# A hybrid encoder layer: the first quarter of x and the first weight tile loaded and split in quarter-megabyte blocks

## The chip, the cores and the metric

One core of one Trainium2 chip runs the whole layer. The metric is device microseconds of one execution, taken as the median of several runs.

## What is computed

The reference, cut to what matters here (batch 1, 256 tokens, width 2048, depth 1):

```
xn = rmsnorm(x, norm_pre_w)                  # 256 x 2048
h  = xn @ w_in                               # 2048 x 13312, split into q, k, v, z, gates ...
...                                          # windowed attention with bias, HGRN2 forward and backward
y  = g_a * (o_a @ w_branch[:1024]) + g_b * (o_b @ w_branch[1024:])
x  = x + rmsnorm(y @ w_out, norm_post_w)
```

The products are kept near float32: each float32 operand is split into a high part, rounded to the type the matmul takes in one pass, and a low part, the remainder. A product is then hi x hi + hi x lo + lo x hi.

## The kernel before, in words

Weights come as "tiles" of 1 MB through the four slots of `raw`. SP issues every weight load in one fixed order (`load`, line 292); a load into a slot waits until VectorE has split the tile that lay there (`lo_ready`). ScalarE copies each half tile (128 x 1024) into `w_hi` (`split_hi`, line 440, the activation is line 447), VectorE subtracts to make `w_lo` (`split_lo`, line 706, line 710). `w_hi` and `w_lo` hold four halves; ScalarE writes a half only when TensorE has counted enough used halves in `half_used`. Each engine runs its own program in order, and all of them meet only at semaphores.

The first 16 tiles are the early tiles. They compute v and i for all heads with the tokens on the rows: tile n covers four of x's sixteen 128-column blocks (k = 4r to 4r+3, r = n mod 4) and 512 output columns, and tiles 0 to 3 together make the first column block of v. Each half tile has two k, two token tiles t and three products each: 12 matmuls of 128 x 512 (lines 1226 to 1228, in `early_tile`, line 1198). In this stage x is used unnormalised apart from the column weights; the row scale is applied when the sums are taken.

x comes from memory with tokens on the partitions. TensorE turns it, 128 x 128 at a time, into PSUM (`turn_x`, line 1186; line 1190). ScalarE makes the high part from PSUM, with the norm's column weight (`first_hi` for k = 0 and 1 by token tile, line 553 and 556; `x_hi` for both token tiles at once, line 559 and 561), and VectorE the low part (`first_lo` line 994, `x_lo` line 1000 and 1002).

The start, engine by engine, in the order of each program:

- SP (lines 335 to 342): x's first 1024 columns for t = 0 (512 KB, `load_x`), the first half of tile 0 (512 KB, `early_half`, line 331), the same two for t = 1 and the second half, tile 1 (1 MB), x's second 1024 columns (two of 512 KB), tiles 2 to 15.
- TensorE (lines 1363 to 1375): six dummy products of ones (`warm`, line 1194), the turn of the norm weights, one dummy, eight turns of x for t = 0, five dummies, eight turns for t = 1, the turn of the vector rows (`ps_vec`, line 1373), then `early_tile(0)` to `early_tile(15)`. A dummy shows as two loads and two matmuls in the trace, a turn as one. In tile 1, between the halves, stand the 16 turns of x's second 1024 columns, which wait for `vec_ready` (the bank they go to is the one the vector rows were in).
- ScalarE (lines 591 to 612): the norm weights from PSUM; for each t, `first_hi(t)` and the high split of half t of tile 0; `x_hi` of k = 2 to 7; the copy of the turned vector rows (line 600, waits for `vec_turned`); the split of tile 1; the squares of x's first columns (line 568); tile 2 with x blocks 8 to 11 between; x blocks 12 to 15; the other squares; from there tile n+1 in step n.
- VectorE (lines 1034 to 1061): the same order for the low parts; later, in steps 6 to 15, the scaled and split activations for the main part (`scale_pair`, lines 1024 and 1027, `act_lo`, line 1031; ScalarE's part is `act_hi`, line 583).
- GpSimd makes the masks at the start, and later adds the column window to the attention bias of each head pair (`mask_bias`, line 409), which SP loads within the group's weight loads.

After the early tiles, weights are the stationary operand (`project`, lines 1173 and 1175) for eight groups of ten tiles, eight tail tiles, 16 branch tiles and 16 output tiles.

Of the kernel before, what the change touches and what calls it, by code (L numbers as in the profile page):

```python
# [25 lines left out]
ALU = mybir.AluOpType  # L26
# [6 lines left out]
P = 128  # L33
# [25 lines left out]
WARM_UP = 6  # L59
KEEP_WARM = 5  # L60
NSLOT_Q, NSLOT_K, NSLOT_Z, NSLOT_F, NSLOT_B, NSLOT_HQ, NSLOT_G0, NSLOT_G1, NSLOT_G2, NSLOT_HZ = range(10)
# [32 lines left out]
def encoder_layer(nc, x, norm_pre_w, w_in, b_gate, na_rel_bias, hg_lb_logits, hg_norm_w, w_branch,  # L94
# [5 lines left out]
    with ExitStack() as ctx:  # L100
# [3 lines left out]
        def sem(name):  # L104
            return ctx.enter_context(nc.semaphore(name))
# [61 lines left out]
        def dec_of(level):  # L167
# [18 lines left out]

        first_landed = [sem(f"first_landed{h}") for h in range(2)]
        raw_landed = [sem(f"raw_landed{i}") for i in range(RAW)]
# [7 lines left out]
            sem("vec_landed"), sem("norm_landed"), sem("norm_turned"), sem("norm_ready"))  # L196
        x_landed = [[sem(f"x_landed{side}{t}") for t in range(2)] for side in range(2)]
        block_taken, v_ready, i_ready = sem("block_taken"), sem("v_ready"), sem("i_ready")
        const_step, ones_ready, win_ready = sem("const_step"), sem("ones_ready"), sem("win_ready")
# [91 lines left out]
        def _(sp):  # L291
# [28 lines left out]

            def load_x(side, t):
                half = slice(side * (D // 2), (side + 1) * (D // 2))
                sp.dma_start(x_tok[:, t, half], x[0, t * P:(t + 1) * P, half]).then_inc(x_landed[side][t], 16)

# [5 lines left out]

            def early_half(h):
                dst = raw[:, 0, 1024 * h:1024 * (h + 1)].rearrange("p (k c) -> p k c", k=2)
                sp.dma_start(dst, w_in_v[:, 2 * h:2 * h + 2, V_TILE * P:V_TILE * P + 512]).then_inc(first_landed[h], 16)

            for t in range(2):
                load_x(0, t)
                early_half(t)
            early(1)
            for t in range(2):
                load_x(1, t)  # L340
            for n in range(2, N_PRE):
# [97 lines left out]
        def _(act):  # L439
            def split_hi(n, r, landed, h):  # L440

                if isinstance(n, int) and n == 0:
                    act.wait_ge(first_landed[h], 16)
                elif h == 0:
# [97 lines left out]
            def group(g0, p, first):  # L542
                g = g0 + p
                for s in range(IN_SLOTS):
# [6 lines left out]
                    take_part(place(g0, p, s)[0], s % 2)  # L551

            def first_hi(t):
                act.wait_ge(xt_done, t + 1)
                for k in range(2):
                    nc.scalar.activation(x_hl[:, k, t * P:(t + 1) * P], first_turned[t][:, k * P:(k + 1) * P], ACT.Copy,
                                         scale=norm_w[:, k:k + 1]).then_inc(xhi_ready, 1)
# [6 lines left out]
            def square(side):  # L564
                wait(act, ss_ready, 2 * side)
                for t in range(2):
                    act.wait_ge(x_landed[side][t], 16)
                    nc.scalar.activation(squares[t], x_tok[:, t, side * (D // 2):(side + 1) * (D // 2)], ACT.Square,
                                         accum_out=ssq[:, 2 * side + t:2 * side + t + 1]).then_inc(ss_ready, 1)
# [24 lines left out]
            for t in range(2):  # L594
                first_hi(t)
                split_hi(0, 0, 0, t)
            for k in range(2, 8):
                x_hi(k)
# [103 lines left out]
        def _(dve):  # L702
# [326 lines left out]
            def act_lo(i):  # L1029
                dve.wait_ge(act_hi_ready, i + 1)  # L1030
                nc.vector.tensor_tensor(act_hl[:, 2 * i:2 * i + 2, T:2 * T], x_pair[i % 2],
                                        act_hl[:, 2 * i:2 * i + 2, 0:T].bitcast(F32), ALU.subtract).then_inc(act_ready, 1)

            dve.wait_ge(norm_ready, 1)
            for t in range(2):
                first_lo(t)
                split_lo(0, 0, t)
            for k in range(2, 8):
                x_lo(k)
# [120 lines left out]
        def _(pe):  # L1160
# [24 lines left out]

            def turn_x(side, t):

                pe.wait_ge(x_landed[side][t], 16)
                for k in range(8 * side, 8 * side + 8):
                    ins = nc.tensor.transpose(turned(k, t), x_tok[:, t, k * P:(k + 1) * P], block[:, 0, :])  # L1190
                    if k == 1 or (t == 1 and k % 2 == 1):
                        ins.then_inc(xt_done, 1)

            def warm(count):
                for _ in range(count):
                    nc.tensor.matmul(ps_proj[1][:, 0:P], ones[:, :], ones[:, :], start=True, stop=True)

            def early_tile(n):

                c, r = n // 4, n % 4  # L1200
                for h in range(2):
                    if (n, h) == (1, 1):
                        pe.wait_ge(vec_ready, 1)
                        for t in range(2):
                            turn_x(1, t)
                    if (n, h) == (5, 1):
# [4 lines left out]
                        ins.then_inc(rows_ready, 1)  # L1211
                    if c == 0 and n + h > 0:
                        pe.wait_ge(xn_ready, 4 * r + 2 * h + 4)
                    elif c > 1 and r == 0 and h == 0:
                        pe.wait_ge(block_taken, 2 * (c - 1))
                    pe.wait_ge(lo_ready, n * 2 + h + 1)
                    i = (2 * r + h) % HALVES
                    for t in range(2):
                        if n + h == 0:
                            pe.wait_ge(xn_ready, 2 * t + 2)  # L1220
# [147 lines left out]
            warm(1)  # L1368
            turn_x(0, 0)
            warm(KEEP_WARM)  # L1370
            turn_x(0, 1)
            pe.wait_ge(vec_landed, 3 * 16)
            nc.tensor.transpose(ps_vec, vec_rows[:, :], block[0:72, 0, 0:72]).then_inc(vec_turned, 1)
            for n in range(N_PRE):
                early_tile(n)
# [82 lines left out]
```

## Time and profile before

| | |
|---|---|
| median of 3 runs | 840.54 us (840.07 to 840.79) |
| profiled execution | 840.67 us |
| its span on the core | 838.9 us |
| TensorE busy | 826.4 us (99%) |
| VectorE busy | 631.9 us (75%) |
| ScalarE busy | 414.0 us (49%) |
| DMA, mean over the span | 183 GB/s |
| mean granted TensorE clock | 0.997 of full speed |

The span is the time between the first and the last record on the core, and the profiled execution's own time is 1.8 us more. Matmuls overlap one another, so a 128 x 512 product shows some 0.39 us busy while one follows another at 0.23 us. All times in the rows are from the start of the span.

### The profile page before, as it was taken

What the parts mean: (1) busy time and instruction counts of PE and PEld (TensorE: products, weight loads), DVE (VectorE), ACT (ScalarE), POOL (GpSimd) and SP (SyncE); (2) the same over time, 40 slices, a digit from 0 to 9 for tenths busy, and PEclk for the clock granted to TensorE, in tenths of its full rate; (3) what the DMA queues carried; (4) which work ended last, traced back from release to release, by engine and by line L of the source; (5) the groups of instructions that cost most, each with busy time, mean ns of one, the idle gap of its engine ahead of it and who ended that gap; (6) DMA issues with size and microseconds to landing.
All of it is one profiled execution on the core that took longest, in us unless ns stands there. A gap on an engine that the chain in (4) does not pass through costs nothing.

```text
span 838.9 us, 14167 instructions
## 1 busy us (share of the span) xinstructions
PE 826.4 (99%) x5006; PEld 708.3 (84%) x5006; DVE 631.9 (75%) x1053; ACT 414.0 (49%) x706; POOL 40.8 (5%) x48
## 2 busy tenths in 40 slices
PE   8999999999999999999999999999999999999996
PEld 7888788888888888888888888888888888888884
DVE  4767658788888888888888897897785778775443
ACT  6644445445445445445445445435545545544442
POOL 5000100000000000000100000100000000000002
PEclk9999999999999999999999999999999999999998
DMA  9755877666566566566567667656557767676522
GB/s 330 273 186 175 209 190 177 174 183 167 161 193 167 158 192 171 154 187 172 160 180 172 167 172 182 166 165 183 152 158 195 215 186 199 185 267 212 185 106 100
DMA packets 246708, 153.63 MB, mean 183 GB/s; under 512 B 15288, under 2 KB 228368, under 8 KB 246288
## 3 DMA queue, kind: packets, MB, share of 16 engines
q1 hardware_dynamic: 245664, 149.17, 63.0%
q10 hardware_dynamic: 1008, 3.98, 1.2%
q8 instruction: 23, 0.38, 0.2%
q14 instruction: 13, 0.11, 0.0%
HBM read 151.04 MB, written 2.10 MB: 183 GB/s over the span
## 4 chain that ended last, share of the span: by engine, by line
PE 91%; DVE 5%; ACT 2%; DMA 1%; issue 1%; POOL 0%; SPq 0%; POOLq 0%; ACTq 0%; DVEq 0%
PE psum L1173 47%; PE psum L1175 23%; PE psum L1414 3%; PE psum L1416 3%; PE psum L1415 3%; DVE w_lo L710 3%; PE psum L1276 2%; PE psum L1226 1%; PE psum L1228 1%; PE psum L1227 1%; ACT w_hi L447 1%; PE psum L1266 1%; DMA raw<-in_w_in 1%; PE psum L1242 1%; PE psum L1311 1%; PE psum L1255 1%
## 5 line engine op out<-in xcount | busy, mean ns | idle before, releaser
L1173 PE MATMUL psum<-act_hl,w_hi 128*128 128x512 f32 x1408 | 502.6, 401 | 0.0
L1175 PE MATMUL psum<-act_hl,w_lo 128*128 128x256 f32 x1408 | 394.9, 280 | 0.0
L710 DVE TENSOR_TENSOR w_lo<-raw,w_hi 128x1024 fp32r<-128x1024 f32 x272 | 325.1, 1233 | 82.5 <-ACT w_hi L447 82.3
L1173 PEld LDWEIGHTS psum<-act_hl,w_hi 128*128 128x128 f32 x1408 | 264.4, 188 | 64.8
L447 ACT ACTIVATE w_hi<-raw 128x1024 fp32r<-128x1024 f32 x272 | 273.6, 1053 | 40.2 <-PE psum L1416 25.6
L1175 PEld LDWEIGHTS psum<-act_hl,w_lo 128*128 128x128 f32 x1408 | 266.0, 189 | 0.0
L461 ACT ACTIVATE part<-psum 128x256 f32<-128x256 f32 x88 | 33.7, 383 | 218.2 <-PE psum L1175 218.1
L1173 PE MATMUL psum<-branch_hl,w_hi 128*128 128x512 f32 x256 | 90.6, 399 | 0.0
L1175 PE MATMUL psum<-branch_hl,w_lo 128*128 128x256 f32 x256 | 71.9, 281 | 0.0
L1173 PEld LDWEIGHTS psum<-branch_hl,w_hi 128*128 128x128 f32 x256 | 48.1, 188 | 12.0
L1226 PE MATMUL psum<-w_hi,branch_hl 128*128 128x512 f32 x128 | 50.4, 393 | 1.5 <-DVE w_lo L710 0.9
L1414 PE MATMUL psum<-w_hi,act_hl 128*128 128x512 f32 x128 | 49.9, 390 | 0.2 <-DVE w_lo L710 0.2
L1228 PE MATMUL psum<-w_hi,branch_hl 128*128 128x512 f32 x128 | 49.8, 389 | 0.0
L1227 PE MATMUL psum<-w_lo,branch_hl 128*128 128x512 f32 x128 | 49.8, 389 | 0.0
L1415 PE MATMUL psum<-w_lo,act_hl 128*128 128x512 f32 x128 | 49.8, 389 | 0.0
L1416 PE MATMUL psum<-w_hi,act_hl 128*128 128x512 f32 x128 | 49.8, 389 | 0.0
L1175 PEld LDWEIGHTS psum<-branch_hl,w_lo 128*128 128x128 f32 x256 | 48.4, 189 | 0.0
L478 ACT ACTIVATE wide<-wide,small 128x256 f32<-128x256 f32 x32 | 16.0, 502 | 47.3 <-DVE small L750 47.3
L731 DVE TENSOR_TENSOR hg<-psum,part 128x256 f32<-128x256 f32 x32 | 13.6, 425 | 31.7 <-ACT part L461 31.7
L790 DVE TENSOR_TENSOR hg<-hg 128x256 f32<-128x256 f32 x56 | 31.8, 568 | 0.8
L1226 PEld LDWEIGHTS psum<-w_hi,branch_hl 128*128 128x128 f32 x128 | 24.0, 188 | 7.3 <-DVE w_lo L710 1.4
L1414 PEld LDWEIGHTS psum<-w_hi,act_hl 128*128 128x128 f32 x128 | 24.0, 188 | 5.5 <-DVE w_lo L710 0.6
(137 smaller groups left out, 691.1 us busy)
## 6 DMA issues: line engine op xcount, KB each, us to landing
raw<-in_w_in SPq DMA_DIRECT2D x103, 1024.0 KB, 5.7
raw<-in_w_branch SPq DMA_DIRECT2D x16, 1024.0 KB, 6.0
raw<-in_w_out SPq DMA_DIRECT2D x16, 1024.0 KB, 5.1
bias_t<-in_na_rel_bias SPq DMA_DIRECT2D x32, 96.0 KB, 5.9
big<-in_x SPq DMA_DIRECT2D x4, 512.0 KB, 8.5
big<-in_x ACTq DMA_DIRECT2D x2, 1024.0 KB, 6.7
out<-big SPq DMA_DIRECT2D x5, 256.0 KB, 2.7
raw<-in_w_in SPq DMA_DIRECT2D x2, 512.0 KB, 6.7
```

Of the source, the lines that this page charges most:

```text
L447: nc.scalar.activation(w_hi[:, (2 * r + h) % HALVES, :], raw[:, r, 1024 * h:1024 * (h + 1)], ACT.Copy).then_inc(hi_ready, 1)
L461: nc.scalar.activation(part[:, b, :], ps_proj[b][:, T:2 * T], ACT.Copy).then_inc(part_ready, 1)
L710: nc.vector.tensor_tensor(w_lo[:, i, :], raw[:, r, 1024 * h:1024 * (h + 1)], w_hi[:, i, :].bitcast(F32), ALU.subtract).then_inc(lo_ready, 1)
L790: hg_s.done(nc.vector.tensor_tensor(sides(suf_f, pre_b, half), sides(suf_f, pre_b, half), sides(pre_f, suf_b, half, 2 * half - 1, 0, 0), A ...
L1173: nc.tensor.matmul(sums[h][:, :], w_hi[:, i, w], operand[:, k, :], start=first, stop=False, skip_group_check=True)
L1175: ins = nc.tensor.matmul(sums[h][:, 0:T], w_lo[:, i, w], operand[:, k, 0:T], start=False, stop=last, skip_group_check=True)
L1226: nc.tensor.matmul(sums, hi, w_hi[:, i, w], start=(k == 0), stop=False)
L1227: nc.tensor.matmul(sums, hi, w_lo[:, i, w], start=False, stop=False)
L1228: ins = nc.tensor.matmul(sums, lo, w_hi[:, i, w], start=False, stop=(k == KT - 1))
L1414: nc.tensor.matmul(o, hi, w_hi[:, i, w], start=(k == 0), stop=False)
L1415: nc.tensor.matmul(o, hi, w_lo[:, i, w], start=False, stop=False)
L1416: ins = nc.tensor.matmul(o, lo, w_hi[:, i, w], start=False, stop=(k == KT - 1))
```

## The change

x's first 1024 columns are loaded as two pieces per token tile: columns 0 to 511, then 512 to 1023. The first weight tile is loaded as four blocks of one k each (128 x 512, 256 KB). SP's order is: x piece one of t = 0, block 0, x piece one of t = 1, blocks 1, 2, 3, x piece two of t = 0 and of t = 1, tile 1, and the rest as before. ScalarE and VectorE split tile 0 block by block. On TensorE a new function, `first_tile`, takes the place of the turns of the first 1024 columns and of `early_tile(0)`: it turns four k instead of eight, has four dummies instead of five, starts the products of block 0 for t = 0 before t = 1 is turned, and turns k = 4 to 7 of both token tiles between the products of blocks 2 and 3. The turn of the vector rows, which stood ahead of all products, stands behind `first_tile`. On ScalarE the order is `first_hi(0)`, block 0, `first_hi(1)`, block 1, x blocks 2 and 3, weight blocks 2 and 3, x blocks 4 to 7, the vector rows' copy, tile 1. The number of products is the same. The square of x's first columns also waits for the new pieces' semaphores.

```diff
-KEEP_WARM = 5
+KEEP_WARM = 4
+FIRST_K = 4
...
             for t in range(2):
-                load_x(0, t)
-                early_half(t)
+                load_x(0, FIRST_K, t, x_first_landed[t])
+                first_weights(t)
+            for k in range(2, FIRST_K):
+                first_weights(k)
+            for t in range(2):
+                load_x(FIRST_K, 8, t, x_landed[0][t])
             early(1)
             for t in range(2):
-                load_x(1, t)
+                load_x(8, KT, t, x_landed[1][t])
...
+            def first_split_hi(k):
+                act.wait_ge(first_landed[k], 16)
+                nc.scalar.activation(w_hi[:, k // 2, 512 * (k % 2):512 * (k % 2) + 512],
+                                     raw[:, 0, 512 * k:512 * (k + 1)],
+                                     ACT.Copy).then_inc(hi_ready if k % 2 else first_w_hi, 1)
...
             for t in range(2):
                 first_hi(t)
-                split_hi(0, 0, 0, t)
-            for k in range(2, 8):
+                first_split_hi(t)
+            for k in range(2, FIRST_K):
+                x_hi(k)
+            for k in range(2, FIRST_K):
+                first_split_hi(k)
+            for k in range(FIRST_K, 8):
                 x_hi(k)
             act.wait_ge(vec_turned, 1)
...
+            def first_split_lo(k):
+                dve.wait_ge(hi_ready if k % 2 else first_w_hi, k // 2 + 1)
+                half = slice(512 * (k % 2), 512 * (k % 2) + 512)
+                nc.vector.tensor_tensor(w_lo[:, k // 2, half], raw[:, 0, 512 * k:512 * (k + 1)],
+                                        w_hi[:, k // 2, half].bitcast(F32),
+                                        ALU.subtract).then_inc(lo_ready if k % 2 else first_w_lo, 1)
+
             dve.wait_ge(norm_ready, 1)
             for t in range(2):
                 first_lo(t)
-                split_lo(0, 0, t)
-            for k in range(2, 8):
+                first_split_lo(t)
+            for k in range(2, FIRST_K):
+                x_lo(k)
+                first_split_lo(k)
+            for k in range(FIRST_K, 8):
                 x_lo(k)
...
+            def first_products(k, t):
+
+                hi, lo = x_hl[:, k, t * P:(t + 1) * P], x_hl[:, k, T + t * P:T + (t + 1) * P]
+                w = slice((k % 2) * 512, (k % 2 + 1) * 512)
+                pe.wait_ge(hi_ready if k % 2 else first_w_hi, k // 2 + 1)
+                pe.wait_ge(xn_ready, 2 * t + 2 if k < 2 else k + 3)
+                nc.tensor.matmul(bank[4 + t], hi, w_hi[:, k // 2, w], start=(k == 0), stop=False)
+                nc.tensor.matmul(bank[4 + t], lo, w_hi[:, k // 2, w], start=False, stop=False)
+                pe.wait_ge(lo_ready if k % 2 else first_w_lo, k // 2 + 1)
+                return nc.tensor.matmul(bank[4 + t], hi, w_lo[:, k // 2, w], start=False, stop=False)
+
+            def first_tile():
+
+                turn_x(0, FIRST_K, 0, x_first_landed[0])
+                warm(KEEP_WARM)
+                first_products(0, 0)
+                turn_x(0, FIRST_K, 1, x_first_landed[1])
+                first_products(0, 1)
+                for t in range(2):
+                    ins = first_products(1, t)
+                ins.then_inc(half_used, 1)
+                for t in range(2):
+                    first_products(2, t)
+                for t in range(2):
+                    turn_x(FIRST_K, 8, t, x_landed[0][t])
+                for t in range(2):
+                    ins = first_products(3, t)
+                ins.then_inc(half_used, 1)
...
             warm(1)
-            turn_x(0, 0)
-            warm(KEEP_WARM)
-            turn_x(0, 1)
+            first_tile()
             pe.wait_ge(vec_landed, 3 * 16)
             nc.tensor.transpose(ps_vec, vec_rows[:, :], block[0:72, 0, 0:72]).then_inc(vec_turned, 1)
-            for n in range(N_PRE):
+            for n in range(1, N_PRE):
                 early_tile(n)
```

## Rows read from the trace of the kernel before

**Rows 1.** The page: the chain that ended last, share of the span by engine.

```profile
PE 91%; DVE 5%; ACT 2%; DMA 1%; issue 1%; POOL 0%; SPq 0%; POOLq 0%; ACTq 0%; DVEq 0%
```

**Rows 2.** Waits of TensorE, 45 us to the end: us in total, times, longest.

```profile
PE psum L1226 <- DVE w_lo L710: 0.9, 1, 0.9
```

**Rows 3.** TensorE's timeline, first 20 us: start, us, operation, xcount, idle before and releaser.

```profile
1.07 2.64 PEld L1196 LDWEIGHTS psum<-ones 128*128 128x128 f32 x12 [1.07 <-POOL ones L366]
...
4.28 0.39 PEld L1196 LDWEIGHTS psum<-ones 128*128 128x128 f32 x2
4.99 0.86 PEld L1190 LDWEIGHTS psum<-block,big 128*128 128x128 f32 x8 [0.32 <-DMA big<-in_x]
5.82 1.20 PEld L1196 LDWEIGHTS psum<-ones 128*128 128x128 f32 x10
8.53 0.85 PEld L1190 LDWEIGHTS psum<-block,big 128*128 128x128 f32 x8 [1.52 <-DMA big<-in_x]
...
9.51 0.49 PE L1226 MATMUL psum<-w_hi,branch_hl 128*128 128x512 f32 x1
...
13.08 0.50 PE L1226 MATMUL psum<-w_hi,branch_hl 128*128 128x512 f32 x1 [0.54 <-DVE branch_hl L1002]
...
15.84 0.19 PEld L1226 LDWEIGHTS psum<-w_hi,branch_hl 128*128 128x128 f32 x1 [0.17 <-issue]
...
18.48 1.90 PEld L1190 LDWEIGHTS psum<-block,big 128*128 128x128 f32 x16
```

**Rows 4.** ScalarE's timeline, first 21 us.

```profile
5.54 0.63 ACT L556 ACTIVATE branch_hl<-psum,vec 128x128 fp32r<-128x128 f32 x2 [0.96 <-PE psum L1190]
7.14 1.06 ACT L447 ACTIVATE w_hi<-raw 128x1024 fp32r<-128x1024 f32 x1 [0.98 <-DMA raw<-in_w_in]
9.01 0.63 ACT L556 ACTIVATE branch_hl<-psum,vec 128x128 fp32r<-128x128 f32 x2 [0.81 <-PE psum L1190]
...
10.85 2.28 ACT L561 ACTIVATE branch_hl<-psum,vec 128x256 fp32r<-128x256 f32 x6
12.99 0.26 ACT L600 ACTIVATE vec<-psum 128x72 f32<-128x72 f32 x1
13.11 2.04 ACT L447 ACTIVATE w_hi<-raw 128x1024 fp32r<-128x1024 f32 x2
...
17.84 1.06 ACT L447 ACTIVATE w_hi<-raw 128x1024 fp32r<-128x1024 f32 x1 [0.62 <-DMA raw<-in_w_in]
20.00 0.84 ACT L561 ACTIVATE branch_hl<-psum,vec 128x256 fp32r<-128x256 f32 x2 [1.09 <-PE psum L1190]
```

**Rows 5.** VectorE's timeline, first 20 us.

```profile
9.66 0.61 DVE L994 SCALAR_TENSOR_TENSOR branch_hl<-psum,vec,branch_hl 128x128 fp32r<-128x128 f32 x2 [0.21 <-ACT branch_hl L556]
...
14.52 2.34 DVE L710 TENSOR_TENSOR w_lo<-raw,w_hi 128x1024 fp32r<-128x1024 f32 x2
18.94 1.23 DVE L710 TENSOR_TENSOR w_lo<-raw,w_hi 128x1024 fp32r<-128x1024 f32 x1 [2.08 <-ACT w_hi L447]
```

**Rows 6.** SP's queue, one of its first issues: start, us, line.

```profile
1.26 0.42 SPq L333 DMA_DIRECT2D raw<-in_w_in  x1
```

**Rows 7.** Groups by form, 30 to 110 us: xcount | busy, mean ns | idle.

```profile
L1031 DVE TENSOR_TENSOR act_hl<-hg,act_hl 128x512 fp32r<-128x512 f32 x8 | 5.5, 684 | 0.0
L583 ACT ACTIVATE act_hl<-hg 128x512 fp32r<-128x512 f32 x8 | 5.1, 633 | 25.6 <-DVE hg L1027 25.6
```

**Rows 8.** The chain that ended last, in order of time: start, us, what.

```profile
45.60 1.07 ACT w_hi L447
```

**Rows 9.** GpSimd's and VectorE's timelines near 89 us.

```profile
88.86 2.41 POOL L409 TENSOR_TENSOR bias_t<-bias_t,win 128x768 f32<-128x768 f32 x1 [57.50 <-DMA bias_t<-in_na_rel_bias]
...
89.49 2.33 DVE L1024 TENSOR_TENSOR hg<-branch_hl 128x512 f32<-128x512 f32 x1
```

**Rows 10.** Stretches at the end: us, busy by engine, granted clock, DMA share, GB/s.

```profile
830.00:835.00 5.00, 0.64 (x3) 0.19 (x1) 4.08 (x8) 2.39 (x5) 4.28 (x4) 0.89 0.65 227
835.00:839.00 4.00, 0.00 (x0) 0.00 (x0) 0.00 (x0) 0.00 (x0) 0.00 (x0) 0.50 0.69 241
```

More of the change, by code:

```diff
@@ L184, in encoder_layer @@
         x_pair = (hg[:, 0:2, :], hg[:, 2:4, :])
-        first_landed = [sem(f"first_landed{h}") for h in range(2)]
+        first_landed = [sem(f"first_landed{k}") for k in range(FIRST_K)]
+        first_w_hi, first_w_lo = sem("first_w_hi"), sem("first_w_lo")
         raw_landed = [sem(f"raw_landed{i}") for i in range(RAW)]
@@ L197, in encoder_layer @@
         x_landed = [[sem(f"x_landed{side}{t}") for t in range(2)] for side in range(2)]
+        x_first_landed = [sem(f"x_first_landed{t}") for t in range(2)]
         block_taken, v_ready, i_ready = sem("block_taken"), sem("v_ready"), sem("i_ready")
@@ L319, in group, with load_x @@
                     load(r, w_in_v[:, :, cols], n)
-            def load_x(side, t):
-                half = slice(side * (D // 2), (side + 1) * (D // 2))
-                sp.dma_start(x_tok[:, t, half], x[0, t * P:(t + 1) * P, half]).then_inc(x_landed[side][t], 16)
+            def load_x(first_k, last_k, t, landed):
+                cols = slice(first_k * P, last_k * P)
+                sp.dma_start(x_tok[:, t, cols], x[0, t * P:(t + 1) * P, cols]).then_inc(landed, 16)
             def early(n):
@@ L329, in early, with first_weights @@
                 load(r, src, n)
-            def early_half(h):
-                dst = raw[:, 0, 1024 * h:1024 * (h + 1)].rearrange("p (k c) -> p k c", k=2)
-                sp.dma_start(dst, w_in_v[:, 2 * h:2 * h + 2, V_TILE * P:V_TILE * P + 512]).then_inc(first_landed[h], 16)
+            def first_weights(k):
+                sp.dma_start(raw[:, 0, 512 * k:512 * (k + 1)],
+                             w_in_v[:, k, V_TILE * P:V_TILE * P + 512]).then_inc(first_landed[k], 16)
             for t in range(2):
-                load_x(0, t)
-                early_half(t)
+                load_x(0, FIRST_K, t, x_first_landed[t])
[4 more added lines that the diff above has]
+                load_x(FIRST_K, 8, t, x_landed[0][t])
             early(1)
             for t in range(2):
-                load_x(1, t)
+                load_x(8, KT, t, x_landed[1][t])
             for n in range(2, N_PRE):
@@ L440, in split_hi @@
             def split_hi(n, r, landed, h):
-                if isinstance(n, int) and n == 0:
-                    act.wait_ge(first_landed[h], 16)
-                elif h == 0:
+                if h == 0:
                     act.wait_ge(raw_landed[r], landed)
@@ L566, in square @@
                 for t in range(2):
+                    if side == 0:
+                        act.wait_ge(x_first_landed[t], 16)
                     act.wait_ge(x_landed[side][t], 16)
@@ L1184, in turned, with turn_x @@
                 return turn_bank[k // 2][:, c:c + P]
-            def turn_x(side, t):
-                pe.wait_ge(x_landed[side][t], 16)
-                for k in range(8 * side, 8 * side + 8):
+            def turn_x(first_k, last_k, t, landed):
+                pe.wait_ge(landed, 16)
+                for k in range(first_k, last_k):
                     ins = nc.tensor.transpose(turned(k, t), x_tok[:, t, k * P:(k + 1) * P], block[:, 0, :])
@@ L1204, in early_tile @@
                         for t in range(2):
-                            turn_x(1, t)
+                            turn_x(8, KT, t, x_landed[1][t])
                     if (n, h) == (5, 1):
@@ L1211, in early_tile @@
                         ins.then_inc(rows_ready, 1)
-                    if c == 0 and n + h > 0:
+                    if c == 0:
                         pe.wait_ge(xn_ready, 4 * r + 2 * h + 4)
@@ L1218, in early_tile @@
                     for t in range(2):
-                        if n + h == 0:
-                            pe.wait_ge(xn_ready, 2 * t + 2)
                         sums = bank[4 + 2 * (c % 2) + t]
```

## The prediction

> **What bounds the kernel now.** I first read the chain of work that ended last [rows 1]: TensorE carries 91% of it, so the body of the kernel is TensorE's own work. The waits of TensorE from 45 us to the end come next [rows 2]: the longest is one of 0.9 us, and no other matters. So nothing behind the start is slack that could swallow a delay or hide a gain, and the question is when TensorE's unbroken work begins. That is in the timelines of the first 20 us, engine by engine. On TensorE [rows 3] the reader is to see three holes: after the warm-up products (5.82 + 1.20 = 7.02) until the turn of x's second token tile at 8.53; then 12 products from 9.51 that end the first half tile; then 0.54 us until 13.08. From 13.08 twelve products take until 15.84, 0.23 us each, and weight tile 1 begins there with a hole of 0.17. ScalarE [rows 4] and VectorE [rows 5] show what feeds this: the weight half is split high in 1.06 us and low in 1.23 us, and x's column blocks are taken from PSUM in 0.38 us each (six in 2.28).
>
> The first low half of tile 1 is ready near 15.75 (two take 2.34 from 14.52, 1.17 apiece) and tile 1 begins at 15.84: before the change TensorE and the split of tile 1 arrive together. That decides this case. The change may start TensorE earlier, but it pays only if tile 1's split is ready earlier too.
>
> **The first blocks, step by step.** Loading: each old 512 KB transfer becomes 256 KB pieces. The pieces have the 2 KB rows that the weight transfers had; the first 2 MB is the same data, in eight issues for four at some 0.46 us each (0.42 and a short gap) [rows 6], so tile 1's issue is about 1.9 us later; tile 1 is wanted by ScalarE only at 15.5, so this costs nothing.
> - Turn of t=0: TensorE is free at 4.28 + 0.39 = 4.67, and now waits for x to 4.99 [rows 3]. With half the bytes I take 4.75 (bounds 4.67 and 4.99). Four turns replace eight, four dummies five; both lie under the wait for the split.
> - ScalarE takes the two blocks 0.5 us after the turn starts, as it did (8.53 to 9.01, 4.99 to 5.54), in 0.63: 5.25 to 5.88. Then the split of weight block 0. No row has exactly this instruction; the nearest of the same size and types are 0.63 on ScalarE and 0.68 on VectorE [rows 7]. High: 5.85 to 6.48. Low: 6.52 to 7.20.
> - Weight block 0 must have landed by 5.85. Its bytes end where x's first 512 KB ended, which had landed by 4.99, and it is issued some 0.46 later: 5.45. Upper bound: the 7.14 of the old half. I take 5.45, so it is hidden.
> - TensorE: two products from 6.55, the low one at 7.22, then the turn of t=1 at 7.45. Its old chain from turn to blocks ready is 8.53 to 9.66 + 0.61 = 10.27 [rows 3, 5], 1.74; plus 0.05: the products of block 0, t=1, begin at 9.24. Three take 0.80 (3 x 0.23, and 0.11 because the first product after a hole shows 0.50 and not 0.39): 10.04. Block 1's six end at 11.42; its low part is ready at 9.9.
> - ScalarE goes on: x blocks 2 and 3 to 9.95, high of weight blocks 2 and 3 to 11.1; VectorE has low 2 ready at 11.2, low 3 at 12.2. So block 2 runs unhindered, 11.42 to 12.80.
>
> Up to here TensorE has done 18 products of tile 0 by 12.80, where it now has done 12. The new order is better than the old by over a microsecond.
>
> **The step that pays it back.** Now x's second quarter is turned, between blocks 2 and 3: eight turns at 1.90 / 16 = 0.12 [rows 3], to 13.74; block 3's six products end at 15.12. Only then comes the turn of the vector rows, which before stood ahead of all products. ScalarE's program has, in order: x blocks 4 to 7, the copy of the vectors, the split of tile 1. Before, all of x's first half was turned by 9.4, and these ran without a wait to the split at 13.11 [rows 4]. Now:
> - x block 4 needs the sixth turn: 12.80 + 0.70, plus the 0.35 that the old row shows (18.48 + 10 x 0.117 = 19.65, ScalarE at 20.00): 13.85. ScalarE idles from 11.1 to there. Four blocks at 0.38: 15.37.
> - The copy of the vectors needs their turn at 15.12, plus 0.3 us until ScalarE has it: 15.42. Both arrive together, so removing either wait alone would not help.
> - Plus 0.12 for the copy: split of tile 1 at 15.54, where it was 13.11. Low starts 1.10 later (17.84 to 18.94 is such a pair), takes 1.23: 17.87. TensorE begins tile 1 at 17.90.
>
> Queued behind on ScalarE: the squares of x, the split of tile 2, x blocks 8 to 15, all shifted alike. Tile 2's transfer, for which ScalarE now waits until 17.84, is hidden then, but the next thing it needs, x block 8, hangs on TensorE's turn behind tile 1's first half, so nothing is caught up. SP's (the load queue's) issues of tiles 4 and on wait for low splits, and shift with them.
>
> **The sum.** 17.90 - 15.84 = +2.06 us at the start of tile 1. From there to 45.6 TensorE has no hole before; at 45.60 the chain passes to ScalarE, released by TensorE's half tile [rows 8], and ScalarE and VectorE set the pace until the 0.9 us wait. In that stretch the 128x512 add on VectorE at 89.49 took 2.33, where a pass of that size takes 0.68 [rows 7]; it ran beside GpSimd's add at 88.86 [rows 9]. Both are timed by the same chain (SP's loads wait for VectorE's splits), so I let the meeting recur unchanged: 0, bounds -0.95 (the wait gone) to +0.8 (a meeting as costly again). So +2.06: 840.67 becomes 842.7 for a profiled execution (span 838.9 to 841.0), and by the median of 840.54, 842.6.
>
> **The clock.** TensorE would stand idle from about 15.4 to 17.9, longer than any hole of the old start (1.5). At the end of the old trace, with 0.64 us of TensorE work in 830 to 835, the granted clock averaged 0.89; in 835 to 839, with none, it was 0.50, which is the 1.2 GHz level [rows 10]. So it falls after idleness, but not at once. At the start the twelve dummy loads take 0.22 each and the later ten 0.12 [rows 3]: the price of the low level is about double. I take no fall, because the work around the hole is dense. The Trainium skill ("TensorE: Matmul & The Clock Gate", section "HAM oscillation — how this bites in real kernels") says that waits between bursts of matmuls send the clock back to half rate and that every return is paid anew; it speaks against this change. Taken at its word here it gives the third rival's time.
>
> **Rivals.**
> 1. *First landing late.* If block 0 lands at 7.14 as the old half did, its split, the turn of t=1 and all that follows come 1.3 us later: +3.3, 843.9. Against: half the bytes are ahead of it. 10%.
> 2. *Part of the cost eased.* The chain from 4.75 to 12.80 is 0.4 shorter, or the meeting with GpSimd clears: +1.1 to +1.6, 841.6 to 842.1. 17%.
> 3. *The clock falls* in the hole: some 3 us of products at half rate, 1.5 lost, +3.6, 844.1. 8%.
> 4. *Faster:* the early start is kept. This needs tile 1's low half by 15.12, the end of block 3; then tile 1 begins 0.72 early: 839.8, and with the GpSimd meeting gone 838.9. It decides where ScalarE starts tile 1's split before 13.5 (15.84 less 1.10, 1.23 and a gap). For it: the first products start near 6.6 instead of 9.51. Against: that split stands in ScalarE's program behind four blocks of x that are not turned before 12.80. 6%, with most of it by a faster first chain than I can derive.
> 5. *Nothing moves* (within a few tenths of 840.5), because the late turn and the early start cancel. Needs the second quarter's turn at 10.7, not 12.80. 5%.
>
> **How the numbers follow.** The forecast has 54%, at +1.7 to +2.5. A measurement of this kernel tells about 0.2%, or 1.7 us, from no change, so my size is only just outside. Slower: the forecast with rivals 1 and 3: 0.72. Same: rivals 2 and 5 and a third of rival 4, whose gain without the meeting is within the bound: 0.24. Faster: the rest of rival 4, 0.04. The range takes in rivals 2 and 1 and reaches to the clock's case: 841.1 to 844.3.
>
> **What would show it.** In the changed trace: first product near 6.6 rather than 9.51; turn of t=1 near 7.45; second quarter's turn near 12.8; ScalarE idle some 2.7 us before x block 4; TensorE's longest hole of the start, 2.5 us, just before tile 1 and released by VectorE's low split; tile 1 at 17.9. From there every row of the old trace should recur 2.1 later. I am wrong if that hole is under 1 us, if the split of tile 1 starts near 13, if the products after 17.9 are spaced at 0.45, or if the wait near 95 changes by more than a few tenths.

## The result, and the profile after

The changed kernel took 843.99 us (median of 5, 842.05 to 844.56), the kernel before 840.60 beside it (840.07 to 841.28): a ratio of 1.0031 (1.0019 to 1.0043). It is slower by 0.3%, which is little, but clear of no change. Measured again later it was 844.06 (843.03 to 844.91) beside 840.62: 1.0043 (1.0029 to 1.0056). The forecast was 842.6, with 841.1 to 844.3 as range. The profiled execution took 842.28, with a span of 840.5.

TensorE's timeline of the changed kernel (start, us, operation, xcount, idle before and what ended it):

```profile
4.73 1.07 PE L1217 MATMUL psum<-block,big 128*128 128x128 f32 x4
5.59 1.50 PE L1223 MATMUL psum<-ones 128*128 128x128 f32 x8
6.96 0.47 PE L1231 MATMUL psum<-w_hi,branch_hl 128*128 128x512 f32 x1
...
7.81 0.60 PE L1217 MATMUL psum<-block,big 128*128 128x128 f32 x4
9.64 0.47 PE L1231 MATMUL psum<-w_hi,branch_hl 128*128 128x512 f32 x1 [1.23 <-DVE branch_hl L1011]
...
13.14 1.03 PE L1217 MATMUL psum<-block,big 128*128 128x128 f32 x8
13.93 0.48 PE L1231 MATMUL psum<-w_hi,branch_hl 128*128 128x512 f32 x1
...
15.39 0.23 PE L1425 MATMUL psum<-block,vec_rows 72*128 72x72 f32 x1
18.24 0.47 PE L1280 MATMUL psum<-w_hi,branch_hl 128*128 128x512 f32 x1 [2.62 <-DVE w_lo L727]
```

Read it beside [rows 3]. The first product stands at 6.96, where it was at 9.51: that part of the change works. From 9.64 on the products and the turn of the second quarter follow without a hole, and tile 0 is done at 15.39. Then the row that matters: tile 1 at 18.24, where it was at 15.84 (its first load; its first product stood at 15.93, so the shift is 2.3 to 2.4), after 2.62 us of nothing, released by VectorE's low split. Whose fault that is, ScalarE's and VectorE's timelines tell:

```profile
9.98 1.16 ACT L560 ACTIVATE w_hi<-raw 128x512 fp32r<-128x512 f32 x2
13.99 1.57 ACT L572 ACTIVATE branch_hl<-psum,vec 128x256 fp32r<-128x256 f32 x4 [2.85 <-PE psum L1217]
15.65 0.23 ACT L617 ACTIVATE vec<-psum 128x72 f32<-128x72 f32 x1
15.78 1.99 ACT L452 ACTIVATE w_hi<-raw 128x1024 fp32r<-128x1024 f32 x2
```

```profile
16.86 2.36 DVE L727 TENSOR_TENSOR w_lo<-raw,w_hi 128x1024 fp32r<-128x1024 f32 x2 [0.34 <-ACT w_hi L452]
```

ScalarE stood idle for 2.85 us, released by TensorE's turn of x, took x blocks 4 to 7 and the vectors, and came to the split of tile 1 at 15.78; in [rows 4] that was at 13.11. The idle time is ScalarE's, but the cause is the place of the turn in TensorE's program.

Near 90 us GpSimd's bias add and VectorE's add meet as they did in [rows 9], and TensorE's only wait from 45 us on is again the one behind it (GpSimd's timeline, VectorE's, and the waits of TensorE):

```profile
91.51 2.13 POOL L416 TENSOR_TENSOR bias_t<-bias_t,win 128x768 f32<-128x768 f32 x1 [57.79 <-DMA bias_t<-in_na_rel_bias]
```

```profile
91.85 2.34 DVE L1041 TENSOR_TENSOR hg<-branch_hl 128x512 f32<-128x512 f32 x1
```

```profile
PE psum L1280 <- DVE w_lo L727: 1.0, 1, 1.0
```

In this execution the shift of +2.4 holds from tile 1 to 703 us and then shrinks little by little to +1.6: the 16 branch tiles took 89.8 us and not 90.5. In the page's groups that is seen as idle time of the weight loads between branch tiles, 12.0 us in the kernel before and 11.3 in this one:

```profile
L1173 PEld LDWEIGHTS psum<-branch_hl,w_hi 128*128 128x128 f32 x256 | 48.1, 188 | 12.0
```

```profile
L1200 PEld LDWEIGHTS psum<-branch_hl,w_hi 128*128 128x128 f32 x256 | 48.0, 188 | 11.3
```

It is no effect of the change: a second profile of the changed kernel shows 12.0 in the same row, and its branch tiles took 90.5 us.

### The profile page after: what moved, and what is told of

Same layout as the page of the kernel before. It is cut to its first block, busy times and chain, and to the rows that moved or that the text cites. A ratio compares the mean times of both kernels' runs of the same rounds, so it can differ in the third digit from the quotient of the medians.

```text
span 840.5 us, 14179 instructions
## 1 busy us (share of the span) xinstructions
PE 826.3 (98%) x5004; PEld 709.1 (84%) x5004; DVE 632.3 (75%) x1055; ACT 414.0 (49%) x708; POOL 40.3 (5%) x48
## 4 chain that ended last, share of the span: by engine, by line
PE 91%; DVE 5%; ACT 2%; issue 1%; POOL 0%; POOLq 0%; ACTq 0%; DVEq 0%
PE psum L1200 47%; PE psum L1202 23%; PE psum L1466 3%; PE psum L1468 3%; PE psum L1467 3%; DVE w_lo L727 3%; PE psum L1330 2%; ACT w_hi L452 1%; PE psum L1280 1%; PE psum L1282 1%; PE psum L1281 1%; PE psum L1320 1%; PE psum L1296 1%; PE psum L1365 1%; PE psum L1309 1%; DVE hg L1041 1%
## 5 line engine op out<-in xcount | busy, mean ns | idle before, releaser
L1200 PE MATMUL psum<-branch_hl,w_hi 128*128 128x512 f32 x256 | 89.8, 396 | 0.0
L1200 PEld LDWEIGHTS psum<-branch_hl,w_hi 128*128 128x128 f32 x256 | 48.0, 188 | 11.3
L1280 PE MATMUL psum<-w_hi,branch_hl 128*128 128x512 f32 x120 | 47.1, 392 | 3.6 <-DVE w_lo L727 3.6
L1281 PE MATMUL psum<-w_lo,branch_hl 128*128 128x512 f32 x120 | 46.7, 389 | 0.0
L1282 PE MATMUL psum<-w_hi,branch_hl 128*128 128x512 f32 x120 | 46.7, 389 | 0.0
L807 DVE TENSOR_TENSOR hg<-hg 128x256 f32<-128x256 f32 x56 | 30.2, 539 | 0.8
L812 DVE TENSOR_TENSOR hg<-hg 128x256 f32<-128x256 f32 x56 | 28.5, 509 | 1.6
```

What stands on the lines that cost most here:

```text
L807: hg_s.done(nc.vector.tensor_tensor(sides(suf_f, pre_b, half), sides(suf_f, pre_b, half), sides(pre_f, suf_b, half, 2 * half - 1, 0, 0), A ...
L1200: nc.tensor.matmul(sums[h][:, :], w_hi[:, i, w], operand[:, k, :], start=first, stop=False, skip_group_check=True)
```

## The experiments

Four questions were open: whether the order of the programs or the small pieces make the delay; which of the two late things, the second quarter or the vector rows, holds the split; whether the clock falls in the hole, which I had given 8%; and what the meeting near 90 us costs. The median of the kernel before, measured beside each, is given each time. It is 839.64 beside four of the kernels and 840.6 to 840.8 beside the others. The kernel before has two levels, near 839.6 and near 840.8, and eight of the fifteen executions behind the 839.64 were at the lower one; what makes the levels is found further down. A difference from 839.64 looks up to 1.1 us larger than one from the upper level.

**Half of the change alone, on the kernel before.** The vector rows are turned behind tile 0's products, nothing else.

```diff
-            pe.wait_ge(vec_landed, 3 * 16)
-            nc.tensor.transpose(ps_vec, ...).then_inc(vec_turned, 1)
-            for n in range(N_PRE):
+            early_tile(0)
+            pe.wait_ge(vec_landed, 3 * 16)
+            nc.tensor.transpose(ps_vec, ...).then_inc(vec_turned, 1)
+            for n in range(1, N_PRE):
```

> The kernel before with one thing changed: the turn of the vector rows behind tile 0's products instead of ahead of them. Order theory: products of tile 0 end near 15.9, then 0.3 to the copy, 0.12, 1.10, 1.23: tile 1 at 18.6, +2.7 us, 843.3 at the lower level; with the clock theory some executions 2 us above that. Theory that the smaller pieces are the cause: no more than +0.5.

Measured: 844.05 (843.77 to 845.50) beside 839.64, ratio 1.0052 (1.0039 to 1.0066). ScalarE's and TensorE's timelines:

```profile
16.39 0.23 ACT L600 ACTIVATE vec<-psum 128x72 f32<-128x72 f32 x1 [3.19 <-PE psum L1374]
16.52 1.99 ACT L447 ACTIVATE w_hi<-raw 128x1024 fp32r<-128x1024 f32 x2
```

```profile
18.97 0.60 PE L1226 MATMUL psum<-w_hi,branch_hl 128*128 128x512 f32 x1 [2.62 <-DVE w_lo L710]
19.37 0.63 PE L1227 MATMUL psum<-w_lo,branch_hl 128*128 128x512 f32 x1
```

The same hole of 2.62 us, without a single small piece: tile 1 3.0 to 3.1 us late (2.7 expected). The order is enough. And the products behind the hole are spaced at 0.40 to 0.43 us and not at 0.23: the clock had fallen in this execution, as the stretch from 17.5 to 21.0 us shows (busy of each engine, granted clock 0.74):

```profile
17.50:21.00 3.50, 2.03 (x5) 1.66 (x6) 2.36 (x2) 3.50 (x7) 0.00 (x0) 0.74 1.06 389
```

None of the five executions came down to the 843.3 that I expected as the lower level; the lowest was 843.77.

**The other half taken away, on the changed kernel.** The vector rows are turned in the hole behind the turn of t=1.

```diff
                 turn_x(0, FIRST_K, 1, x_first_landed[1])
+                pe.wait_ge(vec_landed, 3 * 16)
+                nc.tensor.transpose(ps_vec, ...).then_inc(vec_turned, 1)
...
             first_tile()
-            pe.wait_ge(vec_landed, 3 * 16)
-            nc.tensor.transpose(ps_vec, ...).then_inc(vec_turned, 1)
```

> The changed kernel with the vector rows turned in the hole behind the turn of t=1, not behind block 3. Theory that the late quarter of x and the late vector rows each hold the split of tile 1 (both at 15.4 to 15.65): ScalarE's last x block still ends near 15.6, tile 1 starts at 18.1, time within 0.3 us of the changed kernel's lower level 842.2, with the upper level still there. Theory that the vector rows alone are the cause: split of tile 1 near 13, tile 1 at 15.5, 839.6.

Measured: 844.13 (843.89 to 845.10) beside 839.64. Tile 1 at 18.37, no earlier. ScalarE's and TensorE's timelines:

```profile
14.33 1.57 ACT L572 ACTIVATE branch_hl<-psum,vec 128x256 fp32r<-128x256 f32 x4 [2.87 <-PE psum L1217]
15.77 0.25 ACT L617 ACTIVATE vec<-psum 128x72 f32<-128x72 f32 x1
```

```profile
18.37 0.77 PE L1282 MATMUL psum<-w_hi,branch_hl 128*128 128x512 f32 x1 [2.47 <-DVE w_lo L727]
18.93 0.63 PE L1283 MATMUL psum<-w_lo,branch_hl 128*128 128x512 f32 x1
...
21.42 0.39 PE L1283 MATMUL psum<-w_lo,branch_hl 128*128 128x512 f32 x1
```

The vectors now wait for nothing and still come at 15.77, since x blocks 4 to 7 end there: of two waits that arrive together, the removal of one is worth nothing. All five executions were above the 842.2 that I expected as the lower level, each with a mean clock of 0.995. The stretches (us, busy of each engine, granted clock, DMA share, GB/s) show why:

```profile
15.00:17.50 2.50, 0.90 (x4) 0.38 (x3) 2.16 (x5) 2.50 (x6) 0.00 (x0) 1.00 1.05 386
17.50:21.00 3.50, 2.63 (x6) 2.17 (x7) 1.89 (x3) 3.43 (x6) 0.00 (x0) 0.56 1.05 387
```

TensorE had 0.90 us of work from 15.0 to 17.5, and from 17.5 to 21.0 the granted clock averaged 0.56: nearly all of that stretch at 1.2 GHz. The busy share recovers at once, the clock does not. The same stretches of the changed kernel's profiled execution, whose clock stayed up:

```profile
15.00:17.50 2.50, 0.62 (x4) 0.26 (x2) 2.16 (x5) 2.41 (x5) 0.00 (x0) 1.00 1.05 388
17.50:21.00 3.50, 2.76 (x12) 2.31 (x13) 1.89 (x3) 3.30 (x6) 0.00 (x0) 1.00 1.06 388
```

From the start of tile 1 to that of tile 2 the execution whose clock fell took 8.7 us, the other 7.3: the fall costs 1.4 us. No profile of the changed kernel itself caught a fall.

**The hole filled.** Nine dummy products of ones behind the turn of the vector rows, into a bank that is free then.

```diff
             nc.tensor.transpose(ps_vec, ...).then_inc(vec_turned, 1)
+            for _ in range(9):
+                nc.tensor.matmul(bank[6][:, 256:256 + P], ones[:, :], ones[:, :], start=True, stop=True)
```

> The changed kernel with nine dummy products (into a free bank) right behind the turn of the vector rows, so that TensorE works through its hole before tile 1. They take about 2.2 us and end before the split of tile 1 is ready. Delay theory alone (order on ScalarE, nothing else): tile 1 starts at 18.2 as before, the median stays at 844.0 with executions at both levels, 842.2 and 844.2. Clock theory (the upper level is a clock that falls in the hole): tile 1 starts at 18.2, every execution near 842.2 with mean clock 0.997, median 842.2, and none near 844.

Measured: 843.58 (842.54 to 844.18) beside 839.64. The five mean clocks were 0.997 or 0.998, as the clock theory wants; the times were not all near 842.2 (844.18 had 0.998), so it does not explain all of the scatter. The profiled execution, one of the fastest, shows another part of it (TensorE's, GpSimd's and VectorE's timelines):

```profile
15.67 2.22 PE L1427 MATMUL psum<-ones 128*128 128x128 f32 x18
18.45 0.47 PE L1280 MATMUL psum<-w_hi,branch_hl 128*128 128x512 f32 x1 [0.56 <-DVE w_lo L727]
```

```profile
92.16 2.30 POOL L416 TENSOR_TENSOR bias_t<-bias_t,win 128x768 f32<-128x768 f32 x1 [58.23 <-DMA bias_t<-in_na_rel_bias]
```

```profile
92.07 0.69 DVE L1041 TENSOR_TENSOR hg<-branch_hl 128x512 f32<-128x512 f32 x1
```

The meeting did not happen: VectorE's add began 0.09 us before GpSimd's and took 0.69; in the profile after it began 0.34 behind and took 2.34. From tile 1 to tile 15 this execution took 1.1 us less than the changed kernel's.

**The changed kernel once more**, unaltered.

> The changed kernel again, unaltered, to see its scatter beside the others. Theory: three things come and go beside the fixed +2.3 us at tile 1: the low clock behind the hole (+1.5), the meeting of GpSimd's bias add with VectorE near 90 us (+1.0), and a stretch in the branch tiles that takes 89.9 or 90.6 us. So executions lie between 841.5 and 844.8, those with mean clock 0.995 to 0.996 at the upper end, median 843.3 to 844.2. Rival: the 844 of the first measurement was that chip's alone: median near 842.3.

Measured: 844.06 (843.03 to 844.91) beside 840.62. The three slowest, 844.06, 844.76 and 844.91, had a mean clock of 0.995; the other two, 843.03 and 843.33, had 0.996 and 0.997. The first measurement was no accident. In this profiled execution (843.33, granted clock 1.00 behind the hole) tile 1 stood at 18.59, 0.35 later than in the first profile: x's first piece landed 0.15 later and VectorE's first low split took 0.82 and not 0.68.

**The meeting taken away, on the kernel before.** GpSimd's first bias add is held until the last scaled activation is split.

```diff
+            pool.wait_ge(act_ready, KT // 2)
             mask_bias(0)
```

> The kernel before with GpSimd's first bias add held until the last scaled activation is split (a wait on act_ready 8 ahead of it). Theory that the meeting costs TensorE 1.0 us near 95: VectorE's 2.33 us add is gone, the 0.9 us wait of TensorE is gone, median 839.5, and one of the two levels of the kernel before is missing. Rival (the two levels come from elsewhere): median and spread of the kernel before unchanged, 839.6 to 840.9.

Measured: 839.66 (839.39 to 840.00, 11 executions) beside 840.62 (25 executions: six at 839.4 to 839.7, nineteen at 840.5 to 841.0): ratio 0.9988 (0.9979 to 0.9997). The upper group is gone. GpSimd's timeline and VectorE's:

```profile
95.80 2.76 POOL L409 TENSOR_TENSOR bias_t<-bias_t,win 128x768 f32<-128x768 f32 x1 [64.22 <-DVE act_hl L1032]
```

```profile
89.70 0.68 DVE L1025 TENSOR_TENSOR hg<-branch_hl 128x512 f32<-128x512 f32 x1
```

The 0.9 us wait [rows 2] is gone from TensorE's list. The meeting costs this kernel 1.1 us in most of its executions: the nineteen have a median of 840.71, and the kernel with the held add, which is at the other level in all eleven, 839.66.

**The clock again, with the meeting held off in both.** The changed kernel with the held add, and the same with the nine dummies.

> The changed kernel with GpSimd's first bias add held as in the earlier run, so that the meeting near 90 us no longer blurs the comparison. Clock theory: executions fall into two groups, near 842.0 with mean clock 0.997 (2.3 above the kernel before with the held add, 839.66), and some 1.5 above, near 843.5, with 0.995 to 0.996; the upper group is about half. Rival (low mean clock is only where the record's stretch begins, and costs nothing): one group near 842.0 whatever the clock says.

> As the run before this, with the nine dummies in the hole. Clock theory: one group near 842.1, mean clock 0.997 or more throughout, none above 842.8; median below that of the run before this by 0.5 to 1.5. Rival: same median as the run before this, within 0.3.

Measured, beside 840.75: 843.16 (841.46, 842.25, 842.80, 843.53, 843.65, 844.02) and 842.42 (11 executions, 841.39 to 843.94, ten of them at or below 842.88). With the hole filled the median is 0.7 lower and fewer executions are over 843.5, one of eleven and not three of six. That is the direction of the clock theory, but the executions of the two kernels overlap, and so few don't set the 0.7 clear of noise. It is not the clean split into two groups that I expected, and scatter of 1.5 us is left in a kernel without the long hole or the meeting. The branch tiles (89.8 to 90.7 us in the profiles) are 0.7 to 0.9 of it; what makes them differ I have not found.

**Tile 1 split first.** The first half of tile 1 is split ahead of x blocks 4 to 7.

```diff
+            split_hi(*early_place(1), 0)
             for k in range(FIRST_K, 8):
                 x_hi(k)
             act.wait_ge(vec_turned, 1)
             nc.scalar.activation(vec[:, 0:72], ps_vec, ACT.Copy).then_inc(vec_ready, 1)
-            split_tile(*early_place(1))
+            split_hi(*early_place(1), 1)
...
+            split_lo(1, 1, 0)
             for k in range(FIRST_K, 8):
                 x_lo(k)
-            split_tile(1, 1)
+            split_lo(1, 1, 1)
```

> The changed kernel with tile 1's first half split ahead of x blocks 4 to 7 and of the vectors' copy, on ScalarE and VectorE. Order theory: the split runs near 12.7 in ScalarE's idle time, as soon as tile 1 has landed; tile 1 then waits for the low part of x block 5, near 15.9; hole 0.5 us; time 840.5 (within 0.5), one level, clock 0.997. Theory that the smaller pieces cost by themselves (more issues, more fixed costs, later landing): still 842 or more.

Measured: 841.32 (840.80 to 842.55, 11 executions) beside 839.64, ratio 1.0014 (1.0005 to 1.0023). ScalarE's and TensorE's timelines:

```profile
13.32 1.06 ACT L452 ACTIVATE w_hi<-raw 128x1024 fp32r<-128x1024 f32 x1 [2.17 <-DMA raw<-in_w_in]
```

```profile
16.48 0.50 PE L1282 MATMUL psum<-w_hi,branch_hl 128*128 128x512 f32 x1 [0.83 <-DVE branch_hl L1020]
```

With the pieces kept and two lines moved on two engines, most of the delay is gone: tile 1 at 16.48. That it isn't 15.9 is the load: ScalarE waited for it to 13.32, where I had put the landing at 12.7. The time is 0.8 over the 840.5 that I expected. In the profiled execution another pass of VectorE (line 1049, at 89.53) met GpSimd's add and took 2.33, and TensorE has a wait of 1.0 us behind it.

**The second quarter turned one block earlier**, vector rows early too, GpSimd's add held.

```diff
                 for t in range(2):
-                    first_products(2, t)
-                for t in range(2):
                     turn_x(FIRST_K, 8, t, x_landed[0][t])
+                for t in range(2):
+                    first_products(2, t)
```

> The changed kernel with the second quarter turned between blocks 1 and 2 and the vector rows in the hole behind the turn of t=1, ScalarE's program as the change has it, and the held GpSimd add. Order theory: x block 4 at 13.0 on ScalarE, block 7 done at 14.5, split of tile 1 at 14.7, tile 1 at 17.0 to 17.1, that is 1.2 us later than in the kernel before and 1.1 earlier than the changed kernel; 840.9, clock 0.997. Theory that the split of tile 1 is late for another reason (landing, for one): tile 1 stays at 18.

Measured: 840.17 (839.79 to 841.74, 11 executions), 3.0 below the changed kernel with the held add. ScalarE's and TensorE's timelines:

```profile
12.79 1.57 ACT L573 ACTIVATE branch_hl<-psum,vec 128x256 fp32r<-128x256 f32 x4 [1.52 <-PE psum L1218]
...
14.34 2.03 ACT L453 ACTIVATE w_hi<-raw 128x1024 fp32r<-128x1024 f32 x2
```

```profile
16.83 0.47 PE L1283 MATMUL psum<-w_hi,branch_hl 128*128 128x512 f32 x1 [1.10 <-DVE w_lo L728]
```

Every step is 1.2 to 1.4 us earlier than in the profile after, and the hole is 1.1 us. Beside the kernel that had only the vector rows turned early, this shows that the place of the second quarter's turn, with the vector rows behind it, makes the delay: moving the vector rows alone gained nothing, moving both gained 1.4 us at tile 1. The median fell by twice that, 3.0, and to 0.7 below the 840.9 that I expected. The two profiled executions differ by 1.67 (841.46 and 839.79), close to the 1.55 by which their tile 1 differs (18.38 and 16.83). The other half of the median's gain came with the shorter hole. A clock that falls less often would do it, but no trace here shows that, and the mean clocks don't either: 0.995 to 0.998 with the long hole, 0.996 to 0.998 with the short one, and once 0.948, at 840.00.

**The order mended, with and without the held add.** x's t=1 turned ahead of block 0's products, two dummies and not four, the vector rows and the second quarter early, tile 1 in two loads, its first half split behind x blocks 4 and 5, x blocks 8 to 11 ahead of tile 2's halves, and the second squares behind tile 3's split.

```diff
-KEEP_WARM = 4
+KEEP_WARM = 2
...
-                first_products(0, 0)
                 turn_x(0, FIRST_K, 1, x_first_landed[1])
+                first_products(0, 0)
...
-            early(1)
+            for h in range(2):
+                sp.dma_start(raw[:, 1, 1024 * h:1024 * (h + 1)]...,
+                             w_in_v[:, 4 + 2 * h:6 + 2 * h, ...]).then_inc(
+                                 raw_landed[1] if h else second_landed, 16)
```

> The changed kernel's quarter-megabyte blocks with the order mended: x's t=1 turned ahead of block 0's products (two dummies, not four), vector rows turned behind block 0's first products, second quarter turned between blocks 1 and 2, tile 1 loaded in two halves, its first half split after x blocks 4 and 5, x blocks 8 to 11 taken ahead of tile 2's halves, the second squares behind tile 3's split. Order theory: tile 1 starts near 14.7 to 15.2 (15.84 before), no hole over 1.3 us, mean clock 0.997 in every execution, about 0.7 to 1.1 us faster than the kernel before. Theory that the pieces cost by themselves: no faster than the kernel before, tile 1 at 16 or later.

> The kernel of the run before this one and the held GpSimd add together. If the two gains are independent: 0.7 to 1.1 plus up to 1.0 us faster than the kernel before, and less scatter. If the early start is eaten by another wait: as the held add alone.

Measured, beside 840.62: 840.07 (837.95 to 840.82, 11 executions), ratio 0.9991 (0.9982 to 1.0000), and 838.64 (838.19 to 838.97, 9 executions), ratio 0.9979 (0.9969 to 0.9989). Of the second kernel, ScalarE's and TensorE's timelines:

```profile
11.86 0.84 ACT L577 ACTIVATE branch_hl<-psum,vec 128x256 fp32r<-128x256 f32 x2 [1.96 <-PE psum L1231]
12.67 1.06 ACT L622 ACTIVATE w_hi<-raw 128x1024 fp32r<-128x1024 f32 x1
```

```profile
10.66 1.38 PE L1231 MATMUL psum<-block,big 128*128 128x128 f32 x8
...
15.14 0.47 PE L1296 MATMUL psum<-w_hi,branch_hl 128*128 128x512 f32 x1 [0.34 <-DVE w_lo L738]
```

Tile 1 begins at 15.14, within the 14.7 to 15.2 expected (at 15.45, later than that, in the kernel without the held add, which gained 0.55 and not 0.7 to 1.1, hardly clear of no change), and the longest wait of TensorE from 4 us on is 0.5. With the order mended and GpSimd's add held, the small pieces make a kernel that beats both, by 2.0 us and by 5.4. The pieces and the mended order together add 1.0 us to the held add alone (838.64 against 839.66). How much of this is the pieces is not shown: the same order with the old loads was not run.

## Why the prediction was right, and where it was short

The sign, the mechanism and the place were as forecast, step by step:

| step | forecast | measured |
|---|---|---|
| turn of t=0 | 4.75 | 4.73 |
| first product | 6.55 | 6.96 |
| turn of t=1 | 7.45 | 7.81 |
| block 0, t=1 | 9.24 | 9.64 |
| second quarter's turn | 12.80 | 13.14 |
| ScalarE, x block 4 | 13.85 | 13.99 |
| split of tile 1 | 15.54 | 15.78 |
| tile 1 on TensorE | 17.90 | 18.24 |

The first row is in part luck. In the ten profiles of kernels with the small pieces that turn begins between 4.73 and 5.13, before the change it was at 4.99: half the bytes did not reliably land earlier.

The 0.4 us at the first product come in at two places. The first is my "0.5 us after the turn starts" for ScalarE's first taking. It was 0.74 (4.73 to 5.47), because TensorE's four turns took 1.07 us here and not 0.66, as in the kernel with the vector rows turned early. Their loads took 0.18 us each and not 0.11, which is the low clock of the start (the granted clock reads 1.00 there in both traces, so only the lengths tell). The second place is what the first product waits for. I had it behind ScalarE's split of block 0, which ended at 6.62; it also needs the low part of x from VectorE, done at 6.82, and the dummies ran until 6.90 (TensorE's loads, VectorE, and the same product in the kernel with tile 1 split first, whose dummies ended sooner):

```profile
5.38 1.52 PEld L1223 LDWEIGHTS psum<-ones 128*128 128x128 f32 x8
```

```profile
6.21 0.61 DVE L1011 SCALAR_TENSOR_TENSOR branch_hl<-psum,vec,branch_hl 128x128 fp32r<-128x128 f32 x2 [6.21 <-ACT branch_hl L567]
6.73 0.68 DVE L1054 TENSOR_TENSOR w_lo<-raw,w_hi 128x512 fp32r<-128x512 f32 x1
```

```profile
6.96 0.47 PE L1233 MATMUL psum<-w_hi,branch_hl 128*128 128x512 f32 x1 [0.48 <-DVE branch_hl L1012]
```

The turn of t=1 hangs on VectorE's low split of block 0, which ended at 7.41 where I had 7.20. Of the later steps, x block 4 gave two tenths back (0.85 us behind the start of the second quarter's turn, where I had 1.05), and tile 1 lost one again (2.46 behind its split, not 2.36).

- **Both waits arrive together**: right (x blocks end at 15.6, the vectors' copy starts at 15.65), and shown by the kernels that took one away and gained nothing, and both and gained 1.4 us.
- **Landings are hidden**: right in the changed kernel; ScalarE's split of block 0 at 5.99 follows its x blocks without a wait. Tile 1's landing, 13.3, matters only once the order is mended.
- **No catching up up to 45.6, and the meeting recurs**: right in the profiled execution, +2.4 at tile 1 and at tile 15. Over many executions the meeting comes or not, in the kernel before as well (19 of 25 and 6 of 25 in one measurement), which I had read from one profile as fixed.
- **"I take no fall"**: right in the profiled executions of the changed kernel, not as a rule. Two sister kernels with the same hole show the products behind it at 0.43 us in their traces, both in executions with a mean clock of 0.995. That mean was met in four of ten executions of the changed kernel (843.99, 844.06, 844.76 and 844.91) and in none of the kernel before; that the clock fell in those four is inferred from it and from their times, not seen in a trace. Rival 3 had the price right (1.5; measured 1.4), and its chance, 8%, was too low if they fell. My reason, dense work on both sides of the hole, is what the traces of the sister kernels refute: they had that and fell. The Trainium skill ("TensorE: Matmul & The Clock Gate", section "HAM oscillation — how this bites in real kernels"), which I weighed there, describes such falls for a kernel that waits for loads between its bursts of matmuls, in waits longer than this hole. For this hole the traces of the two sister kernels agree (granted clock 0.56 and 0.74 from 17.5 to 21.0), those of the changed kernel do not (1.00).
- **The size**: +2.06 forecast, +3.4 measured as a difference of medians in both measurements. That is outside the +1.7 to +2.5 to which I gave 54%; the time lies in my range because the range reached to rivals 1 and 3. Rival 1, with nearly the measured time, did not happen: no split waited for block 0. The term that was too small is the shift of tile 1 together with what the hole does behind it. The shift was 2.3 in the first profile and 2.7 in the second (15.93 to 18.59), and there, with the clock up, the meeting and the branch tiles as before the change, it is the whole difference: 843.33 against 840.67. So the order alone costs 2.3 to 2.7. The rest of the 3.4, some 0.7 to 1.1, goes with the long hole, and falls of the clock can make a good part of it: at 1.4 each in four of ten executions they would be 0.6 in the mean (an estimate). The remainder stays open: executions of the changed kernel with a mean clock of 0.996 took up to 844.56.

## What to carry to other kernels

When work on one engine is moved later, read the program of every engine that takes its result: ScalarE's split of the next tile stood behind the copies of the moved turns, and an early start of 2.5 us turned into a late one of 2.4. Ahead of such a change, find what arrives together at the next join (here TensorE and the low split at 15.8) and ask whether both get earlier. A hole costs more than its length if TensorE's clock falls in it. With one and the same hole it fell in some profiles and not in others, so one profile doesn't rule it out.

## What was not expected of the hardware

- **The clock falls in a hole of 2.5 us.** In the kernel with the vector rows turned early TensorE had 0.90 us of work from 15.0 to 17.5 and the clock was at its lower level for most of 17.5 to 21.0, though products ran again from 18.4. In the profiled executions of the changed kernel, with a hole of 2.62, it stayed at 1.00; in the kernel before with only the vector rows late, also with a hole of 2.62, it averaged 0.74 over the same stretch.
- **Who starts first decides, by a tenth of a microsecond.** VectorE's 128x512 add took 2.34 when GpSimd's add had begun 0.34 us earlier, and 0.69 when it began 0.09 ahead of it. In the kernel with the vector rows turned early it began only 0.06 behind, and took 2.33 (GpSimd's and VectorE's timelines):

```profile
93.35 1.84 POOL L416 TENSOR_TENSOR bias_t<-bias_t,win 128x768 f32<-128x768 f32 x1 [58.11 <-DMA bias_t<-in_na_rel_bias]
```

```profile
93.41 2.33 DVE L1041 TENSOR_TENSOR hg<-branch_hl 128x512 f32<-128x512 f32 x1
```

The Trainium skill ("SBUF — State Buffer", section "Who interferes with whom") says that a VectorE instruction with two SBUF inputs contends with a GpSimd instruction that reads SBUF, and that the second to issue blocks until the first is done; these rows agree: the add that came second ended some 0.55 us behind GpSimd's in each of these meetings. Holding a GpSimd instruction that nobody waits for behind the critical stretch was worth 1.0 us in the median for one line.
